# Three moves in a ten-section transformer kernel: stage ends slab by slab, modulation sums in parts, rounded passes in the down product of wide experts

## The reference

```
first_block, layers l = 0, 1:
    m = silu(c) @ w_mod[l] + b_mod[l]                       # 9 vectors of 1024: shift, scale, gate for three sections
    x = x + 0.5*gate0 * swiglu(norm(x)*(1+scale0) + shift0) # feed-forward, 2752 hidden columns
    h = (norm(x)*(1+scale1) + shift1) @ w_in[l]
    mix = windowed attention + gated convolution (l = 0) | rotary attention + long FFT convolution (l = 1)
    x = x + gate1 * (mix @ w_out[l])
    x = x + 0.5*gate2 * swiglu(norm(x)*(1+scale2) + shift2)
second_block, layers l = 0, 1:
    mixer: differential attention, 31-tap convolution, stick-breaking attention; gates; @ w_out
    moe_ffn: 64 experts of 256 hidden columns, 8 of them for each token, and one shared expert:
        out_e = (silu(x_e @ w1[e]) * (x_e @ w3[e])) @ w2[e]
```

## Time and profile before

| | us |
|---|---|
| median of 3 runs | 3786.5 |
| lowest and highest | 3773.27 and 3791.08 |
| the profiled execution, its own time | 3798.87 |
| its span, first to last instruction | 3796.9 |
| PE busy in the span | 3530.8 (93%) |
| DVE busy | 2332.1 (61%) |
| ACT busy | 1477.7 (39%) |
| mean granted TensorE clock | 0.964 of 2.4 GHz |

### The profile page before, as it was taken

The page is one execution under the profiler, slowest core; times in us unless marked ns, Lnnn a source line. Parts: engine busy times, 40 slices in busy tenths (PEclk is TensorE's granted clock), DMA queues, the critical chain, the costliest instruction groups (busy, mean ns, idle before and its releaser), DMA issues.

```text
span 3796.9 us, 52579 instructions
## 1 busy us (share of the span) xinstructions
PE 3530.8 (93%) x21065; PEld 2989.7 (79%) x21065; DVE 2332.1 (61%) x3517; ACT 1477.7 (39%) x2212; POOL 240.3 (6%) x337
## 2 busy tenths in 40 slices
PE   4999899999899998889999999999988999999999
PEld 2997799997699787789767676778778976766776
DVE  6774475775377474546666666656554766666666
ACT  1432233432143204133555555541232355555554
POOL 3010010010001000000000000000000000000000
PEclk9999899999899899889999999999998999999999
DMA  7785286784178552345889998875432688898986
GB/s 260 250 297 165 81 293 196 244 293 152 57 245 303 187 188 100 122 153 183 271 283 292 293 286 283 279 239 171 134 121 90 214 273 270 284 289 274 296 274 191
DMA packets 580320, 842.63 MB, mean 222 GB/s; under 512 B 22715, under 2 KB 489760, under 8 KB 578832
## 3 DMA queue, kind: packets, MB, share of 16 engines
q1 hardware_dynamic: 514508, 665.85, 53.5%
q0 software_dynamic: 41056, 147.35, 11.8%
q10 hardware_dynamic: 24548, 26.57, 2.8%
HBM read 836.37 MB, written 3.33 MB: 221 GB/s over the span
## 4 chain that ended last, share of the span: by engine, by line
PE 77%; DVE 9%; DMA 7%; ACT 3%; issue 2%; SPq 1%; DVEq 0%; ACTq 0%
PE bank L990 14%; PE bank L895 11%; PE bank L896 11%; PE bank L897 11%; PE bank L1336 8%; DMA ring<-in_w 3%; DMA far_up<-in_w 3%; PE bank L1349 2%; PE bank L1306 2%; PE bank L1307 2%; PE bank L1203 2%; PE bank L890 2%; PE bank L1301 2%; PE bank L1303 1%; PE bank L1302 1%
## 5 line engine op out<-in xcount | busy, mean ns | idle before, releaser
L897 PE MATMUL bank<-hh,ring_lo 128*128 128x256 f32 (+1 forms) x2176 | 621.7, 286 | 0.0
L895 PE MATMUL bank<-hh,hi 128*128 128x256 f32 (+1 forms) x1984 | 570.8, 288 | 16.7 <-issue 12.3
L896 PE MATMUL bank<-h_lo,hi 128*128 128x256 f32 (+1 forms) x1984 | 567.0, 286 | 0.0
L990 PE MATMUL bank<-h,ring 128*128 128x256 f32 x2432 | 556.4, 389 | 8.4 <-ACT h L1513 8.4
L990 PEld LDWEIGHTS bank<-h,ring 128*128 128x128 f32 x2432 | 475.7, 196 | 80.2 <-issue 12.1
L897 PEld LDWEIGHTS bank<-hh,ring_lo 128*128 128x128 f32 (+1 forms) x2176 | 419.9, 193 | 0.0
L895 PEld LDWEIGHTS bank<-hh,hi 128*128 128x128 f32 (+1 forms) x1984 | 382.7, 193 | 25.3 <-issue 17.6
L896 PEld LDWEIGHTS bank<-h_lo,hi 128*128 128x128 f32 (+1 forms) x1984 | 382.9, 193 | 0.5 <-issue 0.5
L895 PE MATMUL bank<-hid,hi 128*128 128x256 f32 (+1 forms) x1216 | 346.8, 285 | 2.2 <-DVE ring_lo L2592 2.2
L896 PE MATMUL bank<-hid_lo,hi 128*128 128x256 f32 (+1 forms) x1216 | 343.9, 283 | 0.0
L897 PE MATMUL bank<-hid,ring_lo 128*128 128x256 f32 (+1 forms) x1088 | 307.6, 283 | 0.0
(11 more groups left out here) (372 smaller groups left out, 6642.6 us busy)
## 6 DMA issues: line engine op xcount, KB each, us to landing
ring<-in_w SPq DMA_DIRECT2D x258, 1024.0 KB, 12.3
ring<-in_ffn_w SPq DMA_DIRECT2D x120, 1024.0 KB, 10.5
wmod<-in_w_mod POOLq DMA_DIRECT2D x216, 512.0 KB, 5.6
far_up<-in_w SPq DMA_DIRECT2D x84, 1024.0 KB, 13.1
ring<-in_w_in SPq DMA_DIRECT2D x74, 1024.0 KB, 6.0
work<-in_w SPq DMA_DIRECT2D x42, 1024.0 KB
ring<-in_w_out SPq DMA_DIRECT2D x16, 1024.0 KB, 5.1
ring<-in_w_mod SPq DMA_DIRECT2D x12, 1024.0 KB, 12.7
```

Of the source, the lines that this page charges most:

```text
L895: pe.matmul(o, w_hi, x_hi, start=start, stop=False, skip_group_check=True)
L896: pe.matmul(o, w_hi, x_lo, start=False, stop=False, skip_group_check=True)
L897: return pe.matmul(o, w_lo, x_hi, start=False, stop=stop, skip_group_check=True)
L990: ins = pe.matmul(o[:, half * T:(half + 1) * T], l_, r_, start=(k == 0), stop=(k == KD - 1))
```

## The change

**Mixer ends.** `next_halves` and `add_out` become `end_mixer`. The square root's table is loaded first, then only the first up slab's first half is split before the tiles of the first two `w_out` slabs are added and squared; other halves come next, then the last four tiles. PE takes the first four sums of squares ahead of the last slab. In feed-forward sections the split of the first down slab moves behind the norm.

```diff
+                for c in range(4):
                     linear(slabs[9 + c], 9 + c, taken0, heads=att)
+                    if c == 2:
+                        norm(s + 1, range(4))
...
+            def end_mixer(sec):
...
+                act.activation(idle, eps, ACT.Sqrt)
+                split_up(slots[0:1], 0, lambda j: counts[0], m)
+                squares(s, range(4))
+                act.wait_ge(full[slots[1]], counts[1])
+                act.activation(up_hi(1, 0, m), up_half(slots[1], 0, m), ACT.Copy).then_inc(hi_done, 1)
+                first_halves(nxt, 1)
+                if nxt["kind"] == "moe":
+                    first_halves(nxt, 2)
+                squares(s, range(4, KD))
```

```diff
+            def sum_first(n):
+                pe.wait_ge(mod_step, MOD_STEPS * n)
+                sum_columns(n, SCALE, 0).then_inc(mod_summed, 1)
+                sum_columns(n, SHIFT, 3).then_inc(mod_summed, 1)
+                sum_columns(n, GATE, 1).then_inc(mod_summed, 1)
...
+                    if i == 7 and sec["kind"] == "ab":
+                        pe.wait_ge(proj_taken, taken0 + 6)
+                        sum_mods(s + 1, 5)
...
+                sum_mods(s + 1, 7)
                 pe.wait_ge(*X("prod", 4))
...
-                sum_mods(8 if s == 6 else 9)
                 pe.wait_ge(*X("merged", 1))
```

```diff
-                if s == 6:
-                    act.wait_ge(x_done, KD * (s + 1))
-                    act.dma_start(masks.rearrange("p a t -> p (a t)"), A["k_causal"]).then_inc(masks_in, 16)
                 norm(sec)
                 if s == 1:
+                    more_setup()
                     load_bias()
+                    act.dma_start(masks.rearrange("p a t -> p (a t)"), A["k_causal"]).then_inc(masks_in, 16)
```

```diff
+                            if ORDER[n][0] == "wide":
+                                x_hi, x_lo = few_hi[p % 2][:, c * m:(c + 1) * m], few_lo[:, p % 2, c * m:(c + 1) * m]
+                                pe.matmul(o, x_hi, down_hi(c)[:, d], start=(c == 0), stop=False)
+                                pe.matmul(o, x_hi, low[:, c, d], start=False, stop=False)
+                                ins = pe.matmul(o, x_lo, down_hi(c)[:, d], start=False, stop=(c == 1))
...
                         if gathers(n - 1) and gathers(n - 2):
                             scatter(n - 2)
+                        turn_few(n)
                         finish(n - 1)
-                        turn_few(n)
```

209 lines of the change are left out of this document (135 added, 74 removed).

## The result

The changed kernel takes 3761.1 us at the median (8 runs, 3750.1 to 3772.6) against 3784.7 us for the kernel before (8 runs, 3773.3 to 3791.6): a ratio of 0.9939, 95% interval 0.9918 to 0.9959. It is 23.5 us faster where 58 had been forecast, and outside the range that was given. The profiled execution spans 3770.8 us against 3796.9.

What follows compares the result with a forecast made beforehand. Transfers were taken to bound the kernel inside 15 expert loops and PE outside them. Seams 37.8 us plus experts 20 us (12.8 + 3.6 + 8 - 4.5) made 57.8, hence 3729 us at the median, range 3692 to 3758.

Steps and rivals of the forecast that it cites:

- What bounds the kernel: Expert sections: inside 15 loops of some 20 us transfers are the limit; outside, PE, and all its saved time counts.
- Passes, 12.8 us: Wide down products: three rounded passes save 0.75 us each; loops hide 15 of 32, 17 count, 12.8 us gained.
- first rival: Expert sections: transfers swallow the experts' gain as new loops open; 37.8 us alone is left, 3749 us; chance 0.14.
- turn_few ahead, 3.6 + 8 us: Expert steps: turn_few ahead of finish fills waits for hg, 3.6 us outside the loops and net 8 us inside.
- The splits, -4.5 us: Wide down slabs: added ACT and DVE splits cost 4.5 us, where a dense step directly follows a wide one.
- upper bound of 78 us: Wide down slabs: most the splits could cost, 2.4 us in each of 32 steps if PE's cover were gone.
- third rival: Wide steps: DVE becomes the bound, kernel takes 3807 us, decided from 1.8 us for each wide step; chance 0.06.
- Seams, 37.8 us: Section seams, starts, mixer ends and modulation sums: waits and idle time removed, 37.8 us gained in sum.
- the start of section 1: Section 1: PE's 1.63 us wait for h goes at its start; all terms for the section make 7.6 us.
- the end of section 4: Section 4: sums move into idle time, and the mixer end wins 2.3 us; all terms for the section make 12.8 us.
- Sections 7 and 8: Modulation sums: section 7 loses 2.0 us before the router; section 8's sums cost what they gave, merge wait loses 1.9.
- The signs that I had named: Trace signs across the kernel: product times, waits, norm start, section 4 idle time; sections 7 and 9 shrinking 5 to 20 us each.

Runs made afterwards that it cites:

- e8: Changed kernel with one pass instead of three in the wide down product, low-part passes left out, splits and waits kept: 3750.4 us, ratio 0.9912.
- e10: Kernel of e7 with the wide down slab's splits and the wait on them put back as dead work, product in float32: 3760.7 us, ratio 0.9921.
- e5: The changed kernel unaltered, run again as yardstick on another chip: 3760.6 us, ratio 0.9934 to the kernel before.
- e1: Changed kernel with the experts' part undone: float32 wide down products, turn_few behind finish, no splits of the wide down slab: 3761.2 us, ratio 0.9917.
- e7: Changed kernel with float32 wide down product and no splits of its slab, keeping turn_few ahead of finish: 3747.2 us, ratio 0.9908.
- e9: Kernel of e7 run a second time, no edit, as yardstick on the chip of e10: 3738.5 us, ratio 0.9866.
- e16: Kernel of e7 run a third time, no edit, as yardstick on the chip of e15: 3744.7 us, ratio 0.9889.
- e6: Changed kernel with turn_few behind finish again and the outputs' copies ahead of it, keeping passes and splits: 3778.4 us, ratio 0.9982.
- e15: Kernel of e10 with DVE's two subtractions cut to 8 of 1024 columns, ACT's copies and their waits kept: 3758.2 us, ratio 0.9933.
- e2: Changed kernel with section 8's modulation steps put back from 8, 6 and 6 to 8, 4 and 4: 3749.6 us, ratio 0.9895.

## Why the prediction was wrong, point by point

**What bounds the kernel.** Right as to the loops, wrong in the sentence that outside them "PE is the limit and all of it counts". e8 takes 60 us of PE's work from the wide steps and wins 10. Its trace shows DVE's low parts, `pre` and `hg` right behind a shorter product. I had counted the waits that the trace showed and not asked how near all others were to opening. The earlier trace rows also made the DMA engines look idler than they were: behind the two windows shown there, their share stays at 0.91 to 1.08 for 50 us more, with up to 367 GB/s. And they show DVE busy 4.65 and 6.73 of 10 us, where the prediction has "6.6 of 10 us and more".

**Passes, 12.8 us.** The size of a product was right (0.7 us less, 0.75 forecast). The step that failed is the next one, 17 products that count in full. Beside the splits (e10) the passes bring nothing: 0.9921 without them, 0.9939 and 0.9934 with them. The traces of e10 and of the changed kernel (after and e5) show what takes the place of the 23 us. In the expert steps PE's waits rise from 77.2 us to 91.5 and 89.3, of which before turn_few from 5.1 to 19.2 and 14.5; but for 1.6 us these lead through ACT's split to a transfer that lands. That is the first rival, which had 0.14. What the lower clock level costs, at most, rises from 17.8 us to 30.4 and 24.6; that was in no rival for the experts.

**turn_few ahead, 3.6 + 8 us.** Right within what can be told. e1 against e7's three measurements (0.9917 against 0.9908, 0.9866 and 0.9889) makes 11 us on the mean (3 to 19), and in the profiled executions the two stretches of expert steps take 1726 to 1732 us in e7, e9 and e16 against 1752 in e1, 20 to 26 us less, so the size stays open; beside the passes it is 17.8 (e5 against e6), where it also goes with fewer falls of the clock (11 against 21). The condition I had named, that ACT writes `pre` before `hg` is ready, holds: in the loop shown `pre` is there at 2196.21 and `hg` at 2198.18, just the time that turn_few takes. So a new wait of 19.2 us stands before turn_few, and the old one before the product shrank by 23.9.

**The splits, -4.5 us.** The step that failed most. They cost 22 us (e10 against e9) and 13.5 with DVE's share taken out (e15 against e16). I had costed DVE's list and left ACT's in a line. On ACT the dense slab's split now waits for the wide product, and the `og` copies wait behind it and behind the next up slabs; the third engine to wait is PE at turn_rows, six times 1.43 us. "The dense slab's halves must now wait for the wide down product" stands in the prediction: the list of what is queued behind that wait on ACT does not. My upper bound of 78 us held the truth, the value I took from it did not.

**DVE as the bound of wide steps (third rival).** Right shape, and for this kernel mostly the wrong engine: an engine ahead of PE delays it by its splits, here ACT (e15); DVE does so when the product is shorter still (e8). Its 1.8 us for each wide step was the point of decision; measured are 22 / 32 = 0.7.

**Seams, 37.8 us.** Right in sum. Without the experts' part the kernel is 0.9917 of the one before, 31 us (21 to 42), and the steps' 10 us hide in that: 41 us. That the sum agrees so well is partly luck. In parts they were off both ways: the start of section 1 and the end of section 4 brought less (3.7 for 7.6, 10.6 for 12.8), sections 2 and 6 more, mostly by clock: of the 42.2 us up to section 7, up to 18.8 are time no longer lost at the lower level.

**Sections 7 and 8.** The section 7 sums cost 4.5 us and not 2.0, at the low clock 8.2 us for 48 of them instead of 5.6. For section 8 I had written that sums inside cost what they gave, and lose 1.9. At equal clock, with the steps put back, it loses 2.1 (346.1 before, 348.2 in e2). But the change's (8, 6, 6) was not in my sum: 10 us, and a wait of 10.9 us in the trace. DVE is not busy there, which looked like room; it stands and waits for loads.

**The sum by experiments.** Seams 41, steps -10, turn_few 11, splits and passes -18 to -22: 20 to 24 us, against 23.5 measured. The seams, turn_few and the -18 are differences between neighbours of one row of kernels (e1, e7, the changed one) and add up to the measured gain by themselves; only the -22 (e10 against e9) comes from elsewhere.

**The signs that I had named.** Products at 2.9 us, waits before down products near 30 us, transfers of 13 us in the chain and the norm of section 1 right behind the last product (285.27) all came true. One of the parts did not: idle time was left beside the sums in section 4 (1.17 us). PE waited 15.3 us for the low parts of up slabs, more than "a few us", but it had waited 18.6 in the kernel before, so that sign could say nothing. All these were signs of the parts and not of the sum: the waits had moved one instruction ahead. Only the last, sections 7 and 9 shrinking by 5 to 20 us each, tested the sum: section 7 grew by 8.6 us, and section 9 shrank by 5.1.

## What to carry to other kernels

- When an engine's work is moved or added, write out what stands behind it in order on *that* engine, to the point where another engine waits. Here two copies of 1.06 us on an engine that is 40% busy cost six waits of 1.43 us on PE and some more, and undid a gain of 23 us of PE's time.
- Before counting an engine's saved time in full, find out how far ahead the next inputs are. One kernel with part of the work left out (e8) gives the rate, here one sixth by the medians and one third by the expert steps in the traces, and would have told more than all adding up.
- Check every number in a change, the small ones too: four loads more ahead of a dependent step cost about as much as the best seam won.

## What the runs showed of the hardware that I had not expected

- The granted clock fell to 0.50 behind short waits of PE: 1.43 us (turn_rows), once 0.90 us (a down product, with 0.56 us some two microseconds earlier). A float32 product of 3.64 us then took 5.3, partly at 1.2 GHz, a three-pass one of 2.95 took 4.6, a wide up product of 5.84 took 7.4. Waits of 1.6 to 1.9 us before down products were followed by it 14 times of 26 in e6 and never in 6 in the kernel before. All 14 stood before three-pass products (of 20 such waits) and none before a float32 product (12 such waits, 6 in each kernel). Why isn't settled.
- Because of this the profiled executions of versions whose other sections are alike differ by section: section 1 took 155.3 us (e2) or 149.0 (e10) with the same instructions, 6.3 us apart, with 6.8 us more lost to the low level. A single profile says little about a few microseconds; time at equal clock says more.
- The transfers in the loops of the chain took 9.8 to 16.0 us. Their mean is 13.2 to 13.9 us in every version that has more than two of them: 13.9 in the kernel before, 13.9 with 60 us less work on PE (e8), 13.6 with a freer ACT (e7).
